# Moving work of an attention stage from VectorE and TensorE to GpSimd: the kept x, the summed outputs, and the low parts of two weight slabs

## What is computed

```
qkv = h @ w_qkv
s = einsum('mbhqd,mbhkd->mbhqk', q, k) * scale      # two maps (m) per head
p = softmax(s);  a = p[0] - lam * p[1]
o = einsum('bhqk,bhkv->bhqv', a, v)
o = rmsnorm(o, sub_gain) * (1 - lambda_init)
x = x + o @ w_o
h = rmsnorm(x);  x = x + square(relu(h @ w1)) @ w2
```

## Time and profile before

| what | before |
|---|---|
| median of 3 runs | 992.29 us (992.25 to 992.91) |
| the profiled execution's own time | 991.64 us |
| its span, first to last instruction | 989.8 us |
| PE busy in the span | 975.4 us (99%) |
| DVE busy | 848.8 us (86%) |
| ACT busy | 462.7 us (47%) |
| POOL busy | 352.7 us (36%) |

### The profile page before, as it was taken

How to read it: one execution, slowest core, us unless ns; L and a number is a source line. 1 busy time by engine, 2 the same in 40 slices (tenths; PEclk the granted TensorE clock), 3 DMA queues, 4 the chain that set the end, 5 groups by cost and what they waited for, 6 DMA issues and landing times.

```text
span 989.8 us, 12874 instructions
## 1 busy us (share of the span) xinstructions
PE 975.4 (99%) x4726; PEld 802.6 (81%) x4726; DVE 848.8 (86%) x1122; ACT 462.7 (47%) x711; POOL 352.7 (36%) x317
## 2 busy tenths in 40 slices
PE   9989999989999999999999999999999999999998
PEld 7867778867787888888888888988888888888886
DVE  4785898888887999999999888779998989989883
ACT  6534554666545452443534442475345253552520
POOL 5840455122156538375543200550431503404000
PEclk9999999999999999999999999999999999999999
DMA  7442210130242323333333241303333232422202
GB/s 245 103 127 64 65 65 22 43 128 1 86 147 89 106 86 117 110 101 99 99 114 107 85 132 61 128 1 109 105 114 99 92 120 87 128 86 85 86 1 85
DMA packets 52942, 92.23 MB, mean 93 GB/s; under 512 B 9872, under 2 KB 10896, under 8 KB 52880
## 3 DMA queue, kind: packets, MB, share of 16 engines
q1 hardware_dynamic: 45888, 91.24, 28.7%
q10 hardware_dynamic: 6992, 0.17, 0.4%
HBM read 89.30 MB, written 2.10 MB: 92 GB/s over the span
## 4 chain that ended last, share of the span: by engine, by line
PE 88%; DVE 7%; POOL 2%; issue 1%; DMA 1%; ACT 1%; ACTq 0%; POOLq 0%; DVEq 0%
PE bank L1648 44%; PE pair L1648 40%; PE pair L1709 1%; DVE s_w_lo L1165 1%; PE bank L1709 1%; DMA s_posi<-in_positions 1%; DVE s_nmax L1286 1%; DVE s_acc L1487 0%; DVE s_qkn L1227 0%; DVE s_qk_ss L1213 0%; PE bank L1987 0%; POOL s_ropet L615 0%; ACT s_p L962 0%; DVE s_acc L1525 0%; PE bank L1799 0%
## 5 line engine op out<-in xcount | busy, mean ns | idle before, releaser
L1187 DVE TENSOR_TENSOR s_lbB_lo<-s_lbB,s_b_hi 128x1024 fp32r<-128x1024 f32 x64 | 127.5, 2015 | 0.1
L766 POOL TENSOR_TENSOR s_lt<-s_lbB,s_lbB 128x1024 f32<-128x1024 f32 x14 | 33.6, 2402 | 259.5 <-PE pair L1648 161.7
L1160 DVE TENSOR_TENSOR s_w_lo<-s_raw,s_w_hi 128x1024 fp32r<-128x1024 f32 x72 | 117.8, 1656 | 5.0 <-ACT s_w_hi L846 4.9
L868 ACT ACTIVATE s_b_hi<-s_lbB 128x1024 fp32r<-128x1024 f32 x64 | 67.2, 1053 | 81.3 <-POOL s_lbB L766 38.9
L1648 PE MATMUL bank<-s_hT_hi,s_w_hi 128*128 128x512 f32 x256 | 100.2, 392 | 0.0
L1648 PE MATMUL pair<-s_hT_hi,s_w_hi 128*128 128x512 f32 x256 | 100.1, 391 | 0.0
L1648 PE MATMUL bank<-s_hT_hi,s_w_lo 128*128 128x512 f32 x256 | 99.6, 389 | 0.0
L1648 PE MATMUL pair<-s_hT_hi,s_w_lo 128*128 128x512 f32 x256 | 99.6, 389 | 0.0
L1648 PE MATMUL bank<-s_hT_lo,s_w_hi 128*128 128x512 f32 x256 | 99.6, 389 | 0.0
L1648 PE MATMUL pair<-s_hT_lo,s_w_hi 128*128 128x512 f32 x256 | 99.6, 389 | 0.0
L1021 ACT ACTIVATE s_u_raw<-s_u_raw 128x512 f32<-128x512 f32 x64 | 40.4, 633 | 110.6 <-DVE s_u_raw L1389 110.6
(11 more groups left out here) (262 smaller groups left out, 2681.2 us busy)
## 6 DMA issues: line engine op xcount, KB each, us to landing
s_raw<-in_mlp_w SPq DMA_DIRECT2D x64, 512.0 KB, 3.7
s_lbB<-in_mlp_w SPq DMA_DIRECT2D x64, 512.0 KB, 3.3
s_raw<-in_attn_w_qkv SPq DMA_DIRECT2D x24, 512.0 KB, 3.7
s_raw<-in_attn_w_o SPq DMA_DIRECT2D x8, 512.0 KB, 3.4
s_x_nat<-in_x SPq DMA_DIRECT2D x4, 512.0 KB, 7.8
s_x_again<-in_x SPq DMA_DIRECT2D x4, 512.0 KB, 6.4
out<-s_acc SPq DMA_DIRECT2D x8, 256.0 KB, 2.0
s_raw<-in_pool_w SPq DMA_DIRECT2D x4, 256.0 KB, 2.7
```

Source lines behind the costliest of these rows:

```text
L766: g.tensor_tensor(w2_raw[n][:], w2_raw[one][:], w2_raw[two][:], ALU.subtract).then_inc(t_done, 1)
L868: a.activation(b_hi[home][:], w2_raw[n][:], ACT.Copy).then_inc(w2_hi_done, 1)
L1160: v.tensor_tensor(w_lo[slot][:, cols], raw[k][:], f32(w_hi[slot][:, cols]), ALU.subtract)\
L1187: v.tensor_tensor(w2_lo[n][:], w2_raw[n][:], f32(b_hi[home][:]), ALU.subtract).then_inc(w2_lo_done, 1)
```

## The change

1. The sum `hT_hi + hT_lo`, which is the turned x, is written by POOL to `x_kept` (in place of `hT_hi`) at the steps of `X_SUMMED`, once the projection is done. The second load of x, its 32 transposes and DVE's 8 additions from the bank go; POOL adds `x_kept` to `y_part`, one step after ACT's copy.
2. `o_keep` becomes an ACT copy of bank 5 to `o_parts` and a POOL addition of the two halves. The bank is free after the copy.
3. The fillers of the output projection are cut into parts by head (`W_O_PARTS`); output column 4 takes a fifth head among them, and `w_o_rest` one less.
4. The low parts of slabs 6 and 7 are subtracted by POOL; `SPLIT` moves some pieces of slabs 5, 6 and 7.

```diff
-F_V, F_Y, F_END = 8, 12, 28
+F_V, F_Y, F_END = 8, 12, 20
+W_O_PARTS = (
+    ((19, (0,)), (20, (1,)), (21, (2, 3))),
+    ((19, (0, 1)), (22, (2, 3))),
+    ((23, (0, 1, 2, 3)),),
+    ((25, (0, 1)), (26, (2,)), (27, (3,))),
+    ((27, (0, 1)), (28, (2, 3)), (29, (4,))),
+    ((29, (0, 1, 2)), (30, (3,))),
+    ((30, (0, 1)), (31, (2,)), (32, (3,))),
+    ((31, (0, 1, 2)), (32, (3,))))
+X_SUMMED = (16, 18, 21, 21, 21, 22, 24, 24)
-    w_o = ((18, 22), (20, 22), (24, 24), (25, 26), (27, 28), (28, 29), (31, 31), (32, 32))
-    turned_x = (23, 23, 26, 27, 30, 30, 33, 33)
-SPLIT = {4: (0, 1, 2, 3), 5: (5, 6, 7, 8), 6: (15, 16, 18, 19), 7: (27, 28, 29, 30), 8: (34, 34, 35, 35)}
+SPLIT = {4: (0, 1, 2, 3), 5: (6, 6, 7, 7), 6: (13, 15, 16, 19), 7: (27, 30, 31, 32), 8: (34, 34, 35, 35)}
...
-                sp.dma_start(x_again[:, t, :], xv[:, t, :]).then_inc(x_again_loaded[t], 16)
...
+            def w_o_lo(s, k):
+                pool.wait_ge(w_hi_done, 4 * s + k + 1)
...
+                g.tensor_tensor(w_lo[s % 2][:, cols], raw[k][:], f32(w_hi[s % 2][:, cols]), ALU.subtract)\
+                    .then_inc(w_lo_done, 1)
+            def o_keep(n):
+                h, two = divmod(n, 2)
+                pool.wait_ge(o_copied, n + 1)
...
+                g.tensor_tensor(oc[:, h % 2, 2 * two * VD:(2 * two + 2) * VD].rearrange("p (t d) -> p t d", t=2),
+                                one, other, ALU.add).then_inc(o_kept, 1)
             for i in range(LAST + 1):
+                if i >= 5 and i % 2 and (i - 5) // 2 < 2 * NH:
+                    o_keep((i - 5) // 2)
...
+                for c in range(NC):
+                    if TAKE[F_Y + c] + 1 == i:
+                        pool.wait_ge(y_kept, c + 1)
+                        pool.wait_ge(x_summed, c + 1)
+                        g.tensor_tensor(y_part[:, c, :], y_part[:, c, :], x_kept[:, c, :], ALU.add).then_inc(wo_added, 1)
+                    if X_SUMMED[c] == i:
+                        pool.wait_ge(proj_done, NT * WO0)
+                        g.tensor_tensor(x_kept[:, c, :], f32(hT_hi[:, c, :]), f32(hT_lo[:, c, :]), ALU.add)\
+                            .then_inc(x_summed, 1)
+                for s, steps in SPLIT.items():
+                    for k in range(4):
+                        if steps[k] + 1 == i and s in (WO0, WO0 + 1):
+                            w_o_lo(s, k)
...
+                    act.wait_ge(pv_done, 2 * n + 2)
+                    if n >= 2:
+                        act.wait_ge(o_kept, n - 1)
+                    a.activation(o_parts[:, n % 2, :], bank[5][:], ACT.Copy).then_inc(o_copied, 1)
...
-                v.tensor_reduce(oc[:, h % 2, 2 * pair * VD:(2 * pair + 2) * VD].rearrange("p (t d) -> p t d", t=2),
-                                bank[5][:].rearrange("p (t m d) -> p t d m", t=2, m=2), AX.X, ALU.add)\
-                    .then_inc(o_kept, 1)
...
-                        v.tensor_tensor(y_part[:, c, :], y_part[:, c, :], bank[6 + f % 2][:], ALU.add)\
-                            .then_inc(wo_added, 1)
...
-                    pe.wait_ge(o_kept, i // 2)
+                    pe.wait_ge(o_copied, i // 2)
...
-                        last = nc.tensor.transpose(dst[:, t * P:(t + 1) * P], x_again[:, t, c * P:(c + 1) * P], ident[:])
...
-                    w_o_rest(range(4), (2,))
+                    w_o_rest(range(4), (6,))
                     pe.wait_ge(wo_added, NC)
-                    w_o_rest((6, 7), (0, 1, 2))
+                    w_o_rest((6, 7), (4, 5, 6))
```

More of the change, by code:

```diff
@@ L74 @@
 ADDED = (0, 7, 11, 17)
-F_V, F_Y, F_END = 8, 12, 28
-def y_filler(f):
-    four, k = divmod(f - F_Y, 4)
-    return ("w_o", "x")[k // 2], 2 * four + k % 2
+F_V, F_Y, F_END = 8, 12, 20
[9 more added lines that the diff above has]
+X_SUMMED = (16, 18, 21, 21, 21, 22, 24, 24)
+W_O_DONE = [parts[-1][1][-1] + 1 for parts in W_O_PARTS]
 def filler_steps():
@@ L359, in build_trunk @@
         r_done = sem("r_done")
-        x_turned = sem("x_turned")
+        x_summed = sem("x_summed")
         y_kept = sem("y_kept")
-        x_again_loaded = [sem(f"x_again_loaded{k}") for k in range(NT)]
         x_in_turned = sem("x_in_turned")
@@ L705, in _ @@
             qk_root(2 * NT - 1)
+            def o_keep(n):
+                h, two = divmod(n, 2)
+                pool.wait_ge(o_copied, n + 1)
+                if h >= 2 and two == 0:
+                    pool.wait_ge(side_turned, SIDE_NO["o", h - 2] + 1)
+                one, other = (o_parts[:, n % 2, :].rearrange("p (t m d) -> p t m d", t=2, m=2)[:, :, m, :]
+                              for m in range(2))
+                g.tensor_tensor(oc[:, h % 2, 2 * two * VD:(2 * two + 2) * VD].rearrange("p (t d) -> p t d", t=2),
+                                one, other, ALU.add).then_inc(o_kept, 1)
             for i in range(LAST + 1):
+                if i >= 5 and i % 2 and (i - 5) // 2 < 2 * NH:
+                    o_keep((i - 5) // 2)
                 if i >= 7 and (i - 7) % NT == 0:
@@ L1359, in _ @@
                     for k in range(4):
-                        if steps[k] + 1 == i:
+                        if steps[k] + 1 == i and s not in (WO0, WO0 + 1):
                             split_lo(s, k, s % 2)
@@ L1768, in values, with filler @@
                 last.then_inc(pv_done, 1)
-            def filler(f, half):
+            def filler(f, part):
                 dst = bank[6 + f % 2]
-                if half == 0:
+                if part == 0:
                     g = f - 2
@@ L1779, in filler, with w_o_part, w_o_rest @@
                     elif g >= F_Y:
-                        what, c = y_filler(g)
-                        pe.wait_ge(y_kept if what == "w_o" else wo_added, c + 1)
-                what, c = ("projection", 0) if f < F_Y else y_filler(f)
+                        pe.wait_ge(y_kept, g - F_Y + 1)
+                c = f - F_Y
                 if f < F_Y:
-                    project(NT * AHEAD + f, dst, (2 * half, 2 * half + 1))
-                elif what == "w_o":
-                    for k in (2 * half, 2 * half + 1):
+                    project(NT * AHEAD + f, dst, (2 * part, 2 * part + 1))
+                else:
+                    for k in W_O_PARTS[c][part][1]:
+                        pe.wait_ge(w_lo_done, 4 * WO0 + k + 1)
+                        pe.wait_ge(side_lo_done, SIDE_NO["o", k] + 1)
+                        last = w_o_part(dst, c, k, k == 0, k == W_O_DONE[c] - 1)
+                    if k == W_O_DONE[c] - 1:
+                        last.then_inc(wo_ready, 1)
+            def w_o_part(dst, c, k, start, stop):
+                slot = (WO0 + k // 4) % 2
+                cols = slice(k % 4 * D + c * P, k % 4 * D + (c + 1) * P)
+                return three(dst[:], w_hi[slot][:, cols], w_lo[slot][:, cols], oT[k][:, 0, :], oT[k][:, 1, :],
+                             start, stop)
+            def w_o_rest(cs, ks):
+                for c in cs:
+                    for k in ks:
                         if c == 0:
```

77 lines of the change are left out of this document (26 added, 51 removed).

## The result

The changed kernel takes 994.28 us (median of 14 runs) where the kernel before, run beside it, takes 992.01 (14 runs): 1.0027 times as long, with an interval of 1.0020 to 1.0034. It is slower by some 2.3 us, where the prediction had 0.7 us less. One of the 14 runs of the changed kernel took 4422.1 us, for a reason that no trace shows; the ratio and its interval are taken without it. The profiled execution took 995.17 us with a span of 993.4, against 991.64 and 989.8 before.

What follows compares the result with a forecast made beforehand. PE was taken to bound the kernel, with DVE also near its limit between 188.56 and 291.12 us. 20.4 + 51.0 + 30.5 = 101.9 against 102.56 us, 0.7 less, gave 991.6 us; range 986.6 to 996.0.

Steps and rivals of the forecast that it cites:

- The step that failed: Microseconds PE gains or loses up to 291.12 us, the first MLP's first matmul, reach the end; nothing else does.
- A time moved after 291.12 us: Sign that the prediction is wrong altogether: time changes behind the first matmul of the first MLP.
- One head part fewer: Between column 0's end and the MLP: 0.68 us less cover for DVE's chain, costing 0 to 0.7, taken 0.5.
- A: Steps 17 to 20: forecast 20.4 us, as long as before; 17.6 us at best.
- B: Steps 21 to 31: forecast 51.0 us, against 51.74 before; 48.5 us at best.
- C: The tail, up to the first MLP's first matmul: forecast 30.5 us, against 30.42 before; 27.3 us at best.
- The port's stalls: In each step DVE's mix factor and combine stop until a running POOL instruction ends, which may now take 2.4 us.
- the first rival: Port mostly missed in steps 17 to tail, half the stalls go: 5.2 us less, 987.1 us; chance 0.34.
- Head 6's turn: From step 31, POOL's root stands behind a low part, so PE waits 1.6 to 2.4 us, taken 2.0.
- the half clock: Slow PE clock after the idle time in the tail: would cost 1.4 us, of which half was taken.
- The block on the port: DVE and POOL in SBUF: first to start blocks the other throughout; sharing instead would make the forecast about 4 us lower.
- The second rival: Steps 19 to 20, 31 to 32: o chain behind POOL's low parts, then half clock; 996.5 us, chance 0.26.

Runs made afterwards that it cites:

- e4: Kernel after, with the second low part of the second projection slab one step earlier, in step 30's round in place of step 31's; 990.1 us, ratio 0.9984.
- e6: Kernel after, with the sums of head parts back on DVE as one reduce, without ACT's copy and POOL's addition; 995.96 us, ratio 1.0043.
- e3: Kernel after, with column 4's fifth head part moved from step 29 back to the tail; 988.33 us, ratio 0.9971.
- e2: Kernel before, with POOL's second difference (T3) of block 0 made to wait for DVE's first low part; 995.0 us, ratio 1.0035.
- e7: Kernel after, with both the eight low parts and the sums of head parts back on DVE; 993.23 us, ratio 1.0011.
- e10: Kernel after, with the waits of e1 and e9 both added; 991.74 us, ratio 1.0008.
- e1: Kernel after, with DVE's first low part of block 0 made to wait for POOL's second difference (T3); 993.96 us, ratio 1.0019.
- e11: Kernel after, with the edits of e3 and e4 together; 987.45 us, ratio 0.9951.
- e9: Kernel after, with POOL's fourth difference of block 0 made to wait for DVE's low part of the next weight slab's first piece; 992.5 us, ratio 1.0013.
- e5: Kernel after, with the eight low parts of the two projection slabs back on DVE; 991.33 us, ratio 0.9995.

## Why the prediction was wrong

**The step that failed** is in its first paragraph: that a microsecond up to 291.12 us goes through to the end "and nothing else does". Of the 3.6 us between the spans, 3.4 lie behind the MLP's first matmul. "A time moved after 291.12 us" was its own sign of being wrong altogether. The prediction did see the cause: "One head part fewer stands between column 0's end and the MLP, 0.68 us less cover for DVE's chain there: 0 to 0.7". The shift measured 0.65 us. But I priced it as a delay, at most as long as itself. What it did was to turn the order of two engines on a port, 11 us behind the MLP's first matmul, at 2.66 us. In the profiled execution some 0.8 us more followed behind the first product (675.83 against 675.06 us of rest). It goes with the clock: the three executions with 0.86 or 0.87 there (after, e4, e6) have rests of 675.65 to 675.83 us, the others of 674.69 to 675.06. The rows for it were there before: T3 at 301.93 and DVE's low part at 302.38 stand 0.45 us apart, which is less than 0.68. e3 moves that one part and takes the entry back to 23.62 us; e2 makes the same loss (26.41 us) without the change; e7 has it without the low parts and sums on POOL. Setting both orders right by waits, with the shift still there, gave back 1.67 of the 2.66 us (e10).

**The rest of the sum**, point by point. Forecast for A, B and C: 20.4, 51.0, 30.5, in all 101.9 us; measured 19.61, 50.02, 32.82, in all 102.45. That the total came within 0.6 us is luck: errors of 0.8 and 1.0 us one way and 2.3 the other made up for each other.
- A and B were better by 0.8 and 1.0 us. The port's stalls were rarer than I took: between 170 and 265 us one combine took over 1.4 us (2.36 at 242.21, beside a low part of 2.40), followed as foretold by a late probability of 0.48 us. So in the attention the first rival was nearer to the truth. Steps 21 to 23 and 25 took 4.19, 4.21, 5.11 and 4.54 us, against 4.2, 4.2, 5.1 and 4.2 at best.
- C was worse by 2.3 us. Head 6's turn was foretold with its place, its mechanism (the small product blocked, the root behind the low part) and 1.6 to 2.4 us; it waited 2.49, and the half clock, of which I took 0.7 as half of 1.4, came in full and cost some 1.7. e4 takes both away, 4.36 us. The tail's content was also longer than forecast: step 31 and the tail without that wait take 33.55 us in e4, 28.5 without the 5.09 of step 31, against 27.8 (27.3 and the 0.5 for DVE's chain).
- Head 7's turn had no wait, as forecast (281.40).
- The low part alone took 2.40 us at the median, as forecast, the addition 1.29 (forecast 1.2), the sum 0.74 (0.65), ACT's copy 0.60.
- The block on the port held: the product of 128x4 took 2.35 us beside POOL's 2.85. What the Trainium skill says in SBUF — State Buffer, "Who interferes with whom", agrees with this and with the 3.42 us low parts: the one that comes second gets nothing until the first is through.

The second rival (996.5 us) named the o chain and the clock, and came nearer by the time, but its steps 19 and 20 didn't cost what it said, and it too left the time behind 291.12 untouched. The time of 994.28 lies in the range, but it moved up where the forecast had it go down. The forecast's own range of 989.9 to 993.9 doesn't quite come out of its terms: with the 0.7 us of clock held fixed they give 989.6 to 993.6, and up to 0.8 more with the early steps.

## What to carry to other kernels

Where two engines share a port and the first to come holds it for its whole instruction, look for the pairs of instructions that start close together, also in stages which the change doesn't touch, and compare the gap between them with every shift the change makes: here 0.45 us of lead against 0.65 us of shift was worth 2.7 us. Ask of each engine what its start hangs on: two engines timed by different chains change their order when only one chain moves. And work given to a lightly used engine should be put where nothing on its queue is about to be waited for: the same eight subtractions cost 3 us with the fifth head part in the steps and 0.5, within the noise, with it in the tail.

## What was not expected of the hardware

The same wait has the clock fall in some executions and not in others. Step 20 of the changed schedule has PE without work for 1.83 us ahead of a head's turn. In the kernel after (and e1, e3, e4 and e11) the step ran at full clock, 5.52 to 5.54 us; in the executions of e9 and e10, with the same wait, it did not. The window of the kernel after:

```profile
202.93:208.45 5.52, 3.69 (x25) 2.77 (x26) 4.55 (x9) 3.53 (x7) 4.45 (x4) 1.00 0.04 16
```

and the window of e10:

```profile
203.35:209.88 6.53, 4.69 (x26) 3.72 (x27) 5.31 (x10) 3.54 (x7) 5.46 (x4) 0.83 0.01 4
```

That is 1.0 us by the clock alone. In the kernel before 1.57 us without work were followed by 0.70. The wait of 2.50 us ahead of the first product did the same: a granted clock of 0.86 in the 12.43 us behind it in the kernel after and in e6 and 0.87 in e4, but 1.00 in e2, e5 and e7. What decides between them was not found. The spread between runs goes with it: the changed kernel's run of 993.42 us has a mean clock of 0.998, those of 993.78 to 994.35 one of 0.997, 995.05 and 995.17 one of 0.995, and 996.52 and 996.94 one of 0.993. So an idle time of this length is to be priced with a chance and not with yes or no.

A small instruction's time depends on its neighbour on the other engine: the root of 128x4 on POOL took 1.02 us in the kernel after (306.07), where DVE was waiting for a high part, and 2.01 in the kernel before (304.29), beside DVE's low parts.
